# Re-ordering the w_ada sums and the output norm, and the forget gate inside the score product, in a two-block kernel on one core

## The chip, the cores and the metric

The kernel runs on one NeuronCore of one Trainium2 chip. The metric is the device time of one execution in microseconds (us). Before the change three runs gave 1096.86, 1097.15 and 1097.81 us; the median is 1097.15. About 0.2% is what a measurement can tell from no change.

## The reference

Two transformer-like layers on 256 tokens of width 1024, all in float32. What matters here:

```python
# block 1
ada = silu(c) @ w_ada + b_ada            # 6 vectors of 1024: shift, scale, gate (mixing), shift, scale, gate (FFN)
h  = rmsnorm(x) * (1 + sc1) + sh1
o  = token_mixers(h @ w_in)              # gated scan, 4 heads of 128, and a spatial gating unit (sgu)
     # o_hg = rmsnorm(o_scan) * silu(p_gate);  o_sgu = gelu(u) * (W_s LN(gelu(v)) + b)
x  = x + g1 * (o @ w_out)
h2 = rmsnorm(x) * (1 + sc2) + sh2
x  = x + g2 * conv_ffn(h2)               # w_up to 2 x 2816, 3x3 depthwise conv, gelu, w_down
x  = rmsnorm(x)
# block 2, its attention (8 heads of 64)
s  = (rms(q) . rms(k)) / 8 + cum_f[query] - cum_f[key]     # cum_f = cumsum(log_sigmoid(f))
pr = softmax(where(causal, s, -inf)) ; y = pr @ v
```

The rest of block 2 (a short convolution, a gated delta rule, three gated branches, an FFN, a last gated projection) is not touched.

## The kernel before

**GEMMs.** A weight matrix comes in blocks of 1 MB (1024 x 256), listed in `CHUNKS` in the order of use; SP loads them into a ring of three slots (`raw`). The slot of a block is free when DVE has made its low half. ACT copies a block to `whi` (`split_hi`, L575) and DVE subtracts to get `wlo` (`split_lo`, L584), both in float32r, in rings of three; activations are split in the same way (`hhi`, `hlo`). TensorE (PE) then makes three products for each 128 x 128 tile (L1067 to L1069). A block with 256 tokens is 48 such products ("rows" of the trace). A product in plain float32 shows as two rows.

**Order.** Every engine's program is written out by hand as one list, and semaphores count the steps. An engine that waits holds back all that stands behind it. PSUM banks go round in three lists: `g_units` (banks 0 and 1, GEMMs), `m_units` (banks 2 and 3, small products) and `l_units` (banks 4 to 7). A unit may start only when the unit two (or four) places ahead in its list has been emptied.

**w_ada.** The 24 blocks of w_ada give the six modulation vectors. Blocks 0 to 7 are done first. Blocks 8 to 19 are summed by DVE (`weighted_late`, L1748 to L1765: two scalings, six multiply-adds, one add, in place in the raw slot, then one add into `XC`), each at a set place of DVE's list; four of them make one of the units A2, A3, A4, where PE multiplies by ones to sum over the partitions (`ada_unit`, L1158 to L1166, eight float32 products of one column). Blocks 20 to 23 are summed by POOL (`weighted`, L539 to L547, four tensor operations) while the FFN runs, and PE makes A5 at j = 7. Each block holds a slot of the raw ring until it is summed.

**Mixing.** The scan is worked out in levels 0 to 8 between the GEMMs q, v, mv, mu. At its end come, on PE: first half of mu1, the o products (L1296 to L1301), second half of mu1, gt0, z (spatial product, L1311), the output norm's sums on0 and on1 (L1317), A3, gt1, then w_out (wo0 to wo3), A4, and the sum of squares (L1101) for the FFN's norm. DVE has the w_ada sums 15 and 16, the sgu's norm, z, the reciprocals (L1935) and products of the norm, the low halves (L1929), the splits, sums 17, 18 and 19, and after each wo unit the residual (L1950); ACT follows each residual with the squares (L777) and the next `split_hi`.

**FFN of block 1.** For j in 0 to 10: PE does fg(j), fa(j), down(j-2), 48 rows each; DVE the convolution (L1987, 16 operations) with two splits between, the product with the gelu (L2001), a third split and a low half (L2008). fa(j+1) needs the bank that L2001 empties.

**Scores of block 2.** `fox_scores` (L1427) makes, for each head and each half of the queries, two accumulating products: q with k (L1433), and a selector of 8 rows with the negative cumulated forget gates `NCF` (L1434). FQ holds the queries with the odd heads' rows zeroed, FQO those with the even heads' rows zeroed; FK holds two heads in its 128 rows. DVE takes the maxima (L2143), ACT the exponentials (L904). ACT, DVE and POOL feed this stage from head norms (`unit_norm`, L2103 to L2110).

Of the kernel before, what the change touches and what calls it, by code (L numbers as in the profile page):

```python
# [101 lines left out]
def build(nc, i, out):  # L102
# [91 lines left out]
    for j in range(FFT // 2):  # L194
        g_units += [(f"fg{j}", "act"), (f"fa{j}", "dve")] + [("A5", "dve")] * (j == 7)
# [14 lines left out]
    for lv in range(1, 7):  # L210
# [5 lines left out]
    m_units += [("oA", "act"), ("oB", "act"), ("z0", "dve"), ("z1", "dve"), ("on0", "act"), ("on1", "act"),  # L216
                ("sum1", "act"), ("sum2", "dve"), ("sum3", "dve"), ("sm", "dve"), ("colT", "dve")]
# [3 lines left out]
    with ExitStack() as ctx:  # L221
# [64 lines left out]
        acc_late = slot(12).rearrange("p (b n) -> p b n", b=4)  # L286
# [50 lines left out]
        FQO = h4(13)  # L337
# [101 lines left out]
        var_ready, rstd_ready, weigh_ready = sem("var_ready"), sem("rstd_ready"), sem("weigh_ready")  # L439
        masks_loaded, masks_ready = sem("masks_loaded"), sem("masks_ready")  # L440
        ada_late, keys_summed, vn_used = sem("ada_late"), sem("keys_summed"), sem("vn_used")
        qk_ready, d_raw, d_exp, bg_ready, coef_ready = (
# [12 lines left out]
        def _(sp):  # L455
# [24 lines left out]
            for n, (is_raw, src, (k, w)) in enumerate(CHUNKS):  # L480
# [14 lines left out]
                if is_raw:  # L495
# [7 lines left out]
                    else:  # L503
                        last.append([(ada_pool, c - 19)])
# [24 lines left out]
        def _(pool):  # L529
            pool.memset(eps, EPS).then_inc(pool_step, 1)  # L530
            pool.memset(ones_t, 1.0).then_inc(pool_step, 1)
            steps = [0]

            def link(ins):
                steps[0] += 1
                ins.then_inc(pool_link, 1)
                pool.wait_ge(pool_link, steps[0])

            def weighted(c, dst):  # L539

                n = ada_place[c]
                pool.wait_ge(raw_loaded[n % RING], 16 * (n // RING + 1))
                w = raw[:, n % RING, :].rearrange("p (k n) -> p k n", k=KT)
                link(pool.tensor_tensor(w, w, silu_c[:, :, 0:1].broadcast_to([P, KT, 256]), ALU.mult))
                link(pool.tensor_tensor(w[:, 0:4, :], w[:, 0:4, :], w[:, 4:8, :], ALU.add))
                link(pool.tensor_tensor(w[:, 0:2, :], w[:, 0:2, :], w[:, 2:4, :], ALU.add))
                pool.tensor_tensor(dst, w[:, 0, :], w[:, 1, :], ALU.add).then_inc(ada_pool, 1)  # L547

# [15 lines left out]
            for c in range(20, 24):  # L564
                weighted(c, acc_late[:, c % 4, :])
# [23 lines left out]
        def _(act):  # L589
# [168 lines left out]
            unit_act("gt0", GT[:, 0:2, :], ACT.Silu)  # L758
            split_hi(act, G["gt0"] + RING)
            for n in range(2):  # L760
# [3 lines left out]
                               scale=1.0 / P).then_inc(m_empty["act"], 1)  # L764
            for g, wait in ((2, (sgu_out, 1)), (3, (sgu_out, 2)), (0, (h_f32, 5)), (1, (h_f32, 6))):
# [68 lines left out]
            adv("fd10")  # L834
            link(act.activation(sm_coef[64:68, :], sm_log[64:68, :], ACT.Exp))
# [199 lines left out]
        def _(pe):  # L1035
# [122 lines left out]
            def ada_unit(a):  # L1158

                o = g_open(f"A{a}")  # L1160
                pe.wait_ge(*((ada_late, 4 * (a - 1)) if a < 5 else (ada_pool, 4)))
                for c in range(4 * a, 4 * a + 4):
                    for nb in range(2):
                        at = 2 * (c % 4) + nb
                        src = XC[:, c % 8, :] if a < 5 else acc_late[:, c % 4, :]
# [137 lines left out]
            gemm("mu1", 512, part=(1,))  # L1303
            gemm("gt0", 512)
# [9 lines left out]
            for n in range(2):  # L1314
                o = m_open(f"on{n}")
                pe.wait_ge(osq_ready, n + 1)
                pe.matmul(o[:, :], ones, OSQ[:, 2 * n:2 * n + 2, :].rearrange("p h t -> p (h t)"),  # L1317
                          start=True, stop=True).then_inc(m_full, 1)
# [37 lines left out]

            for j in range(FFT // 2):
# [69 lines left out]
            def fox_scores(u, a, heads):  # L1427
# [988 lines left out]
```

## Time and profile before

| what | value |
|---|---|
| median of 3 runs | 1097.15 us |
| the profiled execution | 1096.29 us, its span 1094.5 us |
| granted clock of TensorE, mean | 0.951 |
| busy: PE, PEld | 1008.1 us (92%), 952.0 us (87%) |
| busy: DVE, ACT, POOL | 783.6 us (72%), 492.5 us (45%), 48.5 us (4%) |
| chain that ended last | PE 62%, DVE 9%, ACT 3%, issue 2%, DMA 1% |
| moved by DMA | 170.56 MB, mean 156 GB/s |

The granted clock is 1 at 2.4 GHz and 0.5 at 1.2 GHz. PE busy is not PE at its peak, since matmuls are pipelined.

### The profile page before, as it was taken

How to read it: one execution, taken by the hardware profiler on the slowest of the kernel's cores; microseconds unless marked ns; L12 is line 12 of the kernel's file. 1: busy time of each engine (PE TensorE's matmuls, PEld its weight loads, DVE VectorE, ACT ScalarE, POOL GpSimd, SP SyncE). 2: the span in 40 equal slices, each digit the busy share in tenths (PEclk: the TensorE clock that was granted, in tenths of full speed). 3: DMA queues.
4: the chain of work that ended last, by engine and by line, in shares of the span. 5: the costliest groups of instructions: out<-in, count | busy, mean ns of one | idle time of the engine just before them, and what ended most of it. 6: DMA issues, size and time to landing. Idle time of an engine off the chain costs nothing.

```text
span 1094.5 us, 17756 instructions
## 1 busy us (share of the span) xinstructions
PE 1008.1 (92%) x7570; PEld 952.0 (87%) x7570; DVE 783.6 (72%) x1090; ACT 492.5 (45%) x587; POOL 48.5 (4%) x35
## 2 busy tenths in 40 slices
PE   5699999888699899969999999999999899999987
PEld 3389999787599899959888589999999799999987
DVE  5668897777989987857959376654486676666664
ACT  5545344425344444437743245232453554454452
POOL 0000000002333300000000000000000000000000
PEclk9899999798899999989998599999999899999999
DMA  9767343364366655645676364734544355555430
GB/s 340 254 222 231 106 162 119 116 205 144 128 218 197 227 179 169 170 101 113 131 167 106 63 132 115 132 95 108 124 154 154 116 186 173 184 191 193 167 104 39
DMA packets 143838, 170.56 MB, mean 156 GB/s; under 512 B 2864, under 2 KB 133184, under 8 KB 143760
## 3 DMA queue, kind: packets, MB, share of 16 engines
q1 hardware_dynamic: 142112, 165.63, 52.1%
q10 hardware_dynamic: 1200, 2.43, 0.6%
q0 software_dynamic: 448, 1.38, 0.4%
q8 instruction: 60, 0.98, 0.4%
q14 instruction: 18, 0.15, 0.0%
HBM read 168.37 MB, written 1.05 MB: 155 GB/s over the span
## 4 chain that ended last, share of the span: by engine, by line
PE 62%; DVE 9%; ACT 3%; issue 2%; DMA 1%; DVEq 0%; ACTq 0%
PE bank L1067 18%; PE bank L1069 17%; PE bank L1068 17%; PE bank L1490 4%; DVE wlo L584 2%; DVE arena L1987 2%; DMA raw<-in_w_in_dram 1%; PE bank L1434 1%; PE bank L1433 1%; ACT whi L575 1%; DVE arena L1669 1%; DVE arena L2067 1%; PE bank L1371 1%; PE bank L1101 1%; DVE arena L2106 1%
## 5 line engine op out<-in xcount | busy, mean ns | idle before, releaser
L1067 PE MATMUL bank<-hhi,whi 128*128 128x256 f32 (+1 forms) x2000 | 589.4, 295 | 54.4 <-ACT hhi L625 14.2
L1068 PE MATMUL bank<-hlo,whi 128*128 128x256 f32 (+1 forms) x2000 | 581.1, 291 | 0.0
L1069 PE MATMUL bank<-hhi,wlo 128*128 128x256 f32 (+1 forms) x2000 | 581.1, 291 | 0.0
L1067 PEld LDWEIGHTS bank<-hhi,whi 128*128 128x128 f32 x2000 | 392.6, 196 | 64.6 <-issue 59.3
L584 DVE TENSOR_TENSOR wlo<-raw,whi 128x2048 fp32r<-128x2048 f32 x131 | 304.5, 2327 | 143.2 <-ACT whi L575 118.2
L1068 PEld LDWEIGHTS bank<-hlo,whi 128*128 128x128 f32 x2000 | 392.5, 196 | 3.9 <-issue 1.2
L1069 PEld LDWEIGHTS bank<-hhi,wlo 128*128 128x128 f32 x2000 | 391.9, 196 | 2.7
L575 ACT ACTIVATE whi<-raw 128x2048 fp32r<-128x2048 f32 x131 | 250.2, 1911 | 113.9 <-PE bank L1069 97.5
L1987 DVE SCALAR_TENSOR_TENSOR arena<-arena,params 128x256 f32<-128x256 f32 x176 | 86.1, 559 | 14.0 <-ACT arena L797 14.0
L2353 DVE SCALAR_TENSOR_TENSOR arena<-bank,params,arena 128x255 f32<-128x255 f32 (+1 forms) x88 | 36.4, 476 | 33.9 <-ACT arena L1000 33.7
L897 ACT ACTIVATE arena<-bank 128x512 f32<-128x512 f32 x22 | 13.2, 598 | 96.6 <-PE bank L1069 96.6
L1000 ACT ACTIVATE arena<-bank,params 128x256 f32<-128x256 f32 x44 | 18.4, 470 | 63.1 <-PE bank L1069 63.1
L1490 PE MATMUL bank<-arena 128*128 128x128 f32 x352 | 41.8, 275 | 1.4 <-DVE arena L2230 1.4
L1490 PEld LDWEIGHTS bank<-arena 128*128 128x128 f32 x352 | 40.6, 192 | 1.6 <-DVE arena L2230 1.6
L1067 PE MATMUL bank<-whi,hhi 128*128 128x256 f32 x128 | 37.1, 290 | 0.0
L1069 PE MATMUL bank<-whi,hlo 128*128 128x256 f32 x128 | 36.2, 283 | 0.0
L1068 PE MATMUL bank<-wlo,hhi 128*128 128x256 f32 x128 | 36.2, 283 | 0.0
L777 ACT ACTIVATE arena<-XT 128x512 f32<-128x512 f32 x16 | 10.0, 631 | 47.9 <-DVE XT L1950 28.4
L1761 DVE SCALAR_TENSOR_TENSOR raw<-raw,small 128x256 f32<-128x256 f32 x72 | 29.5, 477 | 0.0
L2106 DVE RECIPROCAL arena<-arena 128x1024 f32<-128x1024 f32 x4 | 26.2, 6550 | 1.5 <-ACT arena L876 1.4
L806 ACT ACTIVATE arena<-arena 128x512 f32<-128x512 f32 x11 | 7.0, 632 | 42.2 <-DVE arena L1987 42.1
L1067 PEld LDWEIGHTS bank<-whi,hhi 128*128 128x128 f32 x128 | 24.5, 192 | 0.2 <-issue 0.2
(317 smaller groups left out, 933.9 us busy)
## 6 DMA issues: line engine op xcount, KB each, us to landing
raw<-in_w_in_dram SPq DMA_DIRECT2D x46, 1024.0 KB, 8.1
raw<-in_w_up_dram SPq DMA_DIRECT2D x44, 1024.0 KB, 5.1
raw<-in_w_down_dram SPq DMA_DIRECT2D x22, 1024.0 KB, 5.0
raw<-in_w_ada_dram SPq DMA_DIRECT2D x19, 1024.0 KB, 5.2
raw<-in_w_branch_dram SPq DMA_DIRECT2D x6, 1024.0 KB, 5.1
arena<-in_w_ada_dram SPq DMA_DIRECT2D x10, 512.0 KB, 9.0
raw<-in_w_out_dram SPq DMA_DIRECT2D x4, 1024.0 KB, 5.3
raw<-in_w_o_dram SPq DMA_DIRECT2D x4, 1024.0 KB, 5.2
```

Source lines behind the costliest of these rows:

```text
L575: act.activation(whi[:, g % RING, :], raw[:, n % RING, :], ACT.Copy).then_inc(w_hi, 1)
L584: dve.tensor_tensor(wlo[:, g % RING, :], raw[:, n % RING, :], whi[:, g % RING, :].bitcast(F32), ALU.subtract).then_inc(w_lo, 1)
L897: act.activation(dst, two(g_bank(u)), func).then_inc(g_empty["act"], 1)
L1000: ins = act.activation(acc2[:, b, n, t, :], g_bank(f"s{w}{j}")[:, T * t:T * (t + 1)], ACT.Copy, scale=col)
L1067: pe.matmul(o, wh, ah, start=start, stop=False, **kw)
L1068: pe.matmul(o, wh, al, start=False, stop=False, **kw)
L1069: return pe.matmul(o, wl, ah, start=False, stop=stop, **kw)
L1490: ins = pe.matmul(o[:, P * h:P * (h + 1)], lhsT(c, h), rhs(c, h), start=True, stop=True)
L1761: ins = dve.scalar_tensor_tensor(out=w[:, k % 2, :], in0=w[:, k, :], scalar=silu_c[:, k, 0:1], in1=w[:, k % 2, :], op0=ALU.mult, op1=ALU.add)
L1987: ins = dve.scalar_tensor_tensor(out=a, in0=pad[:, b, t, dy:dy + 4, dx:dx + 64], scalar=par("conv_w", k=FFT * tap + 2 * j + t), in1=a, op0 ...
L2106: link(dve.reciprocal(std_, std_))
L2353: ins = dve.scalar_tensor_tensor(out=acc2[:, b, n, t, d:T], in0=ps[:, T * t:T * (t + 1) - d], scalar=par("ffn_conv", k=2 * FFT * (2 - d) + ...
```

## The change

Four things. (1) The raw ring's order and DVE's list: sum 8 goes ahead of a split, sums 13 and 14 go from between the scan's levels to the gate GEMMs, 15 and 16 take their places among the levels, 17 goes ahead of a split after the sgu's norm, 18 and 19 stand each between a residual and a split. (2) on0 and on1 go ahead of gt0 in PE's list and of z in `m_units`; DVE's norm is cut into `unit_length` and `output_gate`. (3) POOL no longer sums: PE multiplies blocks 20 to 23 from the raw slot with `silu_c` itself (`ada_direct`, 16 float32 products of one column for each block), 20 and 21 ahead of fg0, 22 and 23 after fg1 and fg2; A5 becomes an `m_units` entry. (4) `NCF` goes into K: FK_EVEN and FK_ODD each hold one head's rows for k, zeros elsewhere, and in one further row the gate of the head; the queries have ones in that row. POOL clears the two, copies the eight gate rows by DMA and sets the ones; one product for each head and half is left.

```diff
-    for name in ("ff0", "ff1", "fb0", "fb1", 8, 9, "q0", 10, "q1", 11, 12, "v0", "v1", "mv0", 13, "mv1", 14, "mu0",
-                 "mu1", "gt0", "gt1", 15, "wo0", 16, "wo1", "wo2", 17, 18, "wo3", 19):
+    for name in ("ff0", "ff1", "fb0", 8, "fb1", 9, 10, "q0", 11, "q1", 12, 13, 14, "v0", "v1", "mv0", 15, "mv1", 16,
+                 "mu0", "mu1", "gt0", "gt1", 17, "wo0", "wo1", "wo2", 18, "wo3", 19):
...
+                if tag == "f" and j == 1:
+                    ada([21])
                 chunk(f"{tag}g{j}", ...)
+                if tag == "f" and j in (0, 2):
+                    ada([20 + j])
                 chunk(f"{tag}a{j}", ...)
             if j > 1:
                 chunk(f"{tag}d{j - 2}", rows(down, 2 * (j - 2)), (2, D))
-            if tag == "f" and 2 <= j < 6:
-                ada([18 + j])
+            if tag == "f" and j == 2:
+                ada([23])
...
-            for c in range(20, 24):
-                weighted(c, acc_late[:, c % 4, :])
+            pool.memset(FK_EVEN, 0.0).then_inc(fk_zero, 1)
+            pool.wait_ge(m_full, m_no("lk1") + 1)
+            pool.memset(FK_ODD, 0.0).then_inc(fk_zero, 1)
+            pool.wait_ge(rb_ready, 1)
+            pool.wait_ge(fk_zero, 2)
+            for h in range(8):
+                row = (FK_EVEN[64:65, h // 2, :], FK_ODD[0:1, h // 2, :])[h % 2]
+                pool.dma_start(row, NCF[h:h + 1, :]).then_inc(fk_rows, 16)
+            pool.wait_ge(f_ready, 1)
+            pool.memset(FQ[64:65, :, :], 1.0).then_inc(fq_rows, 1)
+            pool.memset(FQO[0:1, :, :], 1.0).then_inc(fq_rows, 1)
...
+            def ada_direct(c):
+                n = ada_place[c]
+                pe.wait_ge(raw_loaded[n % RING], 16 * (n // RING + 1))
+                w = raw[:, n % RING, :].rearrange("p (k n) -> p k n", k=KT)
+                for nb in range(2):
+                    at = 2 * (c % 4) + nb
+                    for k in range(KT):
+                        ins = pe.matmul(m_bank("A5")[:, at:at + 1], w[:, k, P * nb:P * (nb + 1)], silu_c[:, k, 0:1],
+                                        start=k == 0, stop=k == KT - 1)
+                ins.then_inc(m_full if c == 23 else ada_read, 1)
+            ada_direct(20)
+            ada_direct(21)
             for j in range(FFT // 2):
                 gemm(f"fg{j}", T, 8 if j == 0 else None)
+                if j in (1, 2):
+                    ada_direct(21 + j)
                 gemm(f"fa{j}", T)
-                if j == 7:
-                    ada_unit(5)
...
-                    q, k = (FQ, FQO)[h % 2][:, h // 2, P * a:P * (a + 1)], FK[:, h // 2, 0:n]
-                    pe.matmul(o[:, n * m:n * (m + 1)], q, k, start=True, stop=False)
-                    ins = pe.matmul(o[:, n * m:n * (m + 1)], sel(0, h), NCF[0:8, 0:n], start=False, stop=True)
+                    q, k = (FQ, FQO)[h % 2][:, h // 2, P * a:P * (a + 1)], (FK_EVEN, FK_ODD)[h % 2][:, h // 2, 0:n]
+                    ins = pe.matmul(o[:, n * m:n * (m + 1)], q, k, start=True, stop=True)
                 ins.then_inc(l_full, 1)
             pe.wait_ge(f_ready, 2)
+            pe.wait_ge(fk_rows, 128)
+            pe.wait_ge(fq_rows, 2)
```

DVE's list at the end of mixing, after the sgu's norm (the names are those of the code; "sum" is `weighted_late`, "split" is `split_lo`):

```text
before: split(wo0) sum16 split(wo1) z0 z1 modulation3 [norm0 low2 gate0] [norm1 low3 gate1] split(wo2) low0 low1
        sum17 sum18  res0 split(wo3) sum19  res1 split(fg0)  res2 split(fa0)  res3
after:  sum17 split(wo0) norm0 z0 z1 split(wo1) low2 low3 norm1 modulation3 gate0 gate1 low0 low1 split(wo2)
        res0 sum18 split(wo3)  res1 sum19 split(fg0)  res2 split(fa0)  res3
```

DVE's list under the gate GEMMs: before `split sum8 sum9 split decay sum10 split sum11 sum12 split(v0)`, after `sum8 split sum9 sum10 split decay sum11 split sum12 sum13 sum14 split(v0)`. DVE writes K as two operations on 64 partitions each, in place of one on 128. ACT waits for `wsm_zero` before a small exponential, and takes the norm's roots ahead of gt0.

## Rows read from the trace of the kernel before

**Rows 1.** The page, part 2: TensorE's granted clock in 40 slices of 27.4 us, tenths.

```profile
PEclk9899999798899999989998599999999899999999
```

**Rows 2.** Busy time by stretch: start:end, length, then PE, PEld, DVE, ACT, POOL busy (instructions), granted clock, DMA share, GB/s.

```profile
195.00:257.00 62.00, 47.90 (x310) 43.97 (x308) 46.38 (x75) 22.25 (x25) 4.88 (x11) 0.84 0.53 175
257.00:300.00 43.00, 32.02 (x243) 31.11 (x244) 38.12 (x55) 18.15 (x25) 11.29 (x6) 0.90 0.38 118
300.00:400.00 100.00, 96.15 (x766) 95.63 (x765) 92.55 (x115) 45.00 (x50) 31.06 (x12) 0.96 0.63 211
430.00:470.00 40.00, 40.00 (x336) 40.00 (x335) 31.21 (x44) 18.64 (x19) 0.00 (x0) 1.00 0.65 179
...
199.40:213.00 13.60, 12.27 (x45) 10.16 (x46) 8.50 (x13) 3.69 (x5) 0.00 (x0) 0.50 0.45 147
...
602.20:629.40 27.20, 27.20 (x67) 15.66 (x68) 8.69 (x32) 7.06 (x25) 0.00 (x0) 0.50 0.31 62
```

**Rows 3.** Timeline of PE, matmuls: start, time, line, instructions [idle before and its releaser].

```profile
200.73 3.78 PE L1317 MATMUL bank<-arena,cf 128*128 128x512 f32 x4 [3.75 <-DVE arena L1918]
204.30 3.41 PE L1166 MATMUL bank<-cf,XT 128*128 128x1 f32 x16
...
246.29 1.84 PE L1166 MATMUL bank<-cf,XT 128*128 128x1 f32 x16
...
257.33 0.55 PE L1067 MATMUL bank<-hhi,whi 128*128 128x256 f32 x1 [5.38 <-DVE hlo L1684]
...
299.30 0.55 PE L1067 MATMUL bank<-hhi,whi 128*128 128x256 f32 x1 [8.88 <-DVE arena L2001]
```

**Rows 4.** Timeline of DVE, one w_ada sum: its first and its last instruction.

```profile
92.38 0.61 DVE L1758 TENSOR_SCALAR raw<-raw,small 128x256 f32<-128x256 f32 x2
...
95.39 0.43 DVE L1765 TENSOR_TENSOR XT<-raw 128x256 f32<-128x256 f32 x1
```

**Rows 5.** Timeline of DVE at the end of mixing: a split, a reciprocal, a split, the last residual.

```profile
191.96 2.29 DVE L584 TENSOR_TENSOR wlo<-raw,whi 128x2048 fp32r<-128x2048 f32 x1 [4.58 <-ACT whi L575]
...
207.84 3.34 DVE L1935 RECIPROCAL arena<-arena 128x512 f32<-128x512 f32 x1
...
241.39 2.29 DVE L584 TENSOR_TENSOR wlo<-raw,whi 128x2048 fp32r<-128x2048 f32 x1 [2.56 <-issue]
...
249.23 0.87 DVE L1950 SCALAR_TENSOR_TENSOR XT<-bank,mod,XT 128x256 f32<-128x256 f32 x2
```

**Rows 6.** Timeline of ACT: the high half of block v0.

```profile
99.04 1.91 ACT L575 ACTIVATE whi<-raw 128x2048 fp32r<-128x2048 f32 x1
```

**Rows 7.** The page, part 6: loads of w_in, KB each, median us to landing.

```profile
raw<-in_w_in_dram SPq DMA_DIRECT2D x46, 1024.0 KB, 8.1
```

**Rows 8.** Timeline at the FFN's start: POOL's multiplication, and DVE's split beside it.

```profile
283.09 3.93 POOL L544 TENSOR_TENSOR raw<-raw,small 128x2048 f32<-128x2048 f32 x1 [25.17 <-DMA raw<-in_w_ada_dram]
...
287.22 4.48 DVE L584 TENSOR_TENSOR wlo<-raw,whi 128x2048 fp32r<-128x2048 f32 x1
```

**Rows 9.** The chain that ended last, in order of time: start, us, engine, line.

```profile
471.46 0.89 DVE XT L1950 x2
...
623.02 1.15 PE bank L1434 x2
...
685.46 1.78 PE bank L1490 x16
...
848.57 3.47 PE bank L1101 x16
```

**Rows 10.** Timeline of the scores: the first product, then the weight loads of two later ones.

```profile
597.63 0.38 PE L1433 MATMUL bank<-arena 128*128 128x128 f32 x2
...
614.89 0.50 PEld L1433 LDWEIGHTS bank<-arena 128*128 128x128 f32 x2 [0.65 <-issue]
...
616.05 0.50 PEld L1434 LDWEIGHTS bank<-arena,XT 8*128 8x128 f32 x2 [0.65 <-issue]
```

**Rows 11.** Waits of the whole span: total us, times, longest us.

```profile
DVE arena L2143 <- PE bank L1434: 19.3, 6, 3.8
```

More of the change, by code:

```diff
@@ L503, in _ @@
                     else:
-                        last.append([(ada_pool, c - 19)])
+                        last.append([(ada_read, c - 19) if c < 23 else (m_full, m_no("A5") + 1)])
                     n_ada = max(n_ada + 1, 8) if n_ada >= 5 else n_ada + 1
@@ L764, in _ @@
                                scale=1.0 / P).then_inc(m_empty["act"], 1)
+            unit_act("gt0", GT[:, 0:2, :], ACT.Silu)
+            split_hi(act, G["gt0"] + RING)
             for g, wait in ((2, (sgu_out, 1)), (3, (sgu_out, 2)), (0, (h_f32, 5)), (1, (h_f32, 6))):
@@ L834, in _ @@
             adv("fd10")
+            act.wait_ge(wsm_zero, 3)
             link(act.activation(sm_coef[64:68, :], sm_log[64:68, :], ACT.Exp))
@@ L1303, in _ @@
             gemm("mu1", 512, part=(1,))
+            for n in range(2):
+                o = m_open(f"on{n}")
+                pe.wait_ge(osq_ready, n + 1)
+                pe.matmul(o[:, :], ones, OSQ[:, 2 * n:2 * n + 2, :].rearrange("p h t -> p (h t)"),
+                          start=True, stop=True).then_inc(m_full, 1)
             gemm("gt0", 512)
@@ L1313, in _ @@
                 ins.then_inc(m_full, 1)
[L1314 to L1318, printed above, removed]
             ada_unit(3)
@@ L1868, in _ @@
             level(2)
-            weighted_late(13)
+            weighted_late(15)
             values(0, 1)
@@ L1908, in _, with mixed_low, unit_length, output_gate @@
             dve.tensor_tensor(MV, MV, sgu_b.unsqueeze(1).broadcast_to([P, 2, 512]), ALU.add).then_inc(vn_ready, 1)
+            weighted_late(17)
             split_lo(dve, G["mu1"] + RING)
-            weighted_late(16)
-            split_lo(dve, G["gt0"] + RING)
+            def mixed_low(g):
+                dve.wait_ge(h_hi, 4 + (3, 4, 1, 2)[g])
+                s = slice(2 * g, 2 * g + 2)
+                dve.tensor_tensor(mix_lo[:, s, :], OM[:, s, :], mix_hi[:, s, :].bitcast(F32), ALU.subtract
+                                  ).then_inc(h_lo, 1)
+            def unit_length(n):
+                s = slice(2 * n, 2 * n + 2)
+                dve.wait_ge(*m_done(f"on{n}"))
+                link(dve.reciprocal(hrstd[:, s, :], hstd[:, s, :]))
+                link(dve.tensor_tensor(OM[:, s, :], OM[:, s, :], hrstd[:, s, :], ALU.mult))
+            def output_gate(n):
+                dve.wait_ge(*g_done(f"gt{n}"))
+                for h in (2 * n, 2 * n + 1):
+                    ins = dve.scalar_tensor_tensor(out=OM[:, h, :], in0=OM[:, h, :], scalar=par("hg_norm", k=h),
+                                                   in1=GT[:, h, :], op0=ALU.mult, op1=ALU.mult)
+                ins.then_inc(h_f32, 1)
+            unit_length(0)
             for n in range(2):
@@ L1923, in _ @@
                 dve.tensor_tensor(o, o, U[:, 2 * n:2 * n + 2, :], ALU.mult).then_inc(sgu_out, 1)
+            split_lo(dve, G["gt0"] + RING)
+            mixed_low(2)
+            mixed_low(3)
+            unit_length(1)
             modulation(3, g_wait("A3"), g_empty["dve"])
-            def mixed_low(g):
-                dve.wait_ge(h_hi, 4 + (3, 4, 1, 2)[g])
-                s = slice(2 * g, 2 * g + 2)
-                dve.tensor_tensor(mix_lo[:, s, :], OM[:, s, :], mix_hi[:, s, :].bitcast(F32), ALU.subtract
-                                  ).then_inc(h_lo, 1)
-            for n in range(2):
-                s = slice(2 * n, 2 * n + 2)
-                dve.wait_ge(*m_done(f"on{n}"))
-                link(dve.reciprocal(hrstd[:, s, :], hstd[:, s, :]))
-                link(dve.tensor_tensor(OM[:, s, :], OM[:, s, :], hrstd[:, s, :], ALU.mult))
-                mixed_low(2 + n)
-                if n == 1:
-                    dve.wait_ge(*g_done("gt1"))
-                for h in (2 * n, 2 * n + 1):
-                    ins = dve.scalar_tensor_tensor(out=OM[:, h, :], in0=OM[:, h, :], scalar=par("hg_norm", k=h),
-                                                   in1=GT[:, h, :], op0=ALU.mult, op1=ALU.mult)
-                ins.then_inc(h_f32, 1)
-            split_lo(dve, G["gt1"] + RING)
+            output_gate(0)
+            output_gate(1)
             mixed_low(0)
             mixed_low(1)
+            split_lo(dve, G["gt1"] + RING)
             def residual(nb, ps, gate):
@@ L2009, in _ @@
                                   ).then_inc(u_lo, 1)
-                if j == 7:
-                    modulation(5, g_wait("A5"), g_empty["dve"])
+                if j == 3:
+                    dve.wait_ge(m_full, m_no("A5") + 1)
+                    modulation(5, m_bank("A5"), m_empty["dve"])
             split_lo(dve, G["fd9"] + RING)
             dve.wait_ge(down_used, FFT // 2)
+            dve.wait_ge(*m_done("A5"))
             for c in range(4):
@@ L2133, in _ @@
             dve.wait_ge(*g_done("fk1"))
-            unit_norm(FK, fk_std, "sfk1", par("fox_gain", k=1), f_ready)
+            dve.wait_ge(*m_done("sfk1"))
+            dve.wait_ge(fk_zero, 2)
+            link(dve.reciprocal(fk_std, fk_std))
+            for dst, r in ((FK_EVEN, slice(0, 64)), (FK_ODD, slice(64, 128))):
+                ins = dve.scalar_tensor_tensor(out=dst[r, :, :], in0=FK[r, :, :], scalar=par("fox_gain", k=1)[r, :],
+                                               in1=fk_std[r, :, :], op0=ALU.mult, op1=ALU.mult)
+            ins.then_inc(f_ready, 1)
             adv("scc0")
```

48 lines of the change are left out of this document (17 added, 31 removed).

## Prediction

> **What bounds the kernel now.** I read the page first, where the clock slices are lowest at about 600 us [rows 1], then the busy time by stretch, then the gaps of TensorE in the timeline. TensorE is the bound: in the middle of the first block's FFN it is busy without a break, 336 rows in 40.00 us, so 0.119 us for one row of a GEMM [rows 2]. The time that can be won is therefore what TensorE loses elsewhere: in waits, and in stretches where the granted clock is at 1.2 instead of 2.4 GHz. By stretch: the end of mixing (195 to 257 us) has 14.1 us without a matmul and clock 0.84; the FFN's start (257 to 300) 11.0 us without one; 300 to 400 us another 3.9; and 602 to 629 us runs wholly at the half clock though PE never stops [rows 2].
>
> **End of mixing.** PE waits 3.75 us for DVE before the output norm's sums (L1317), because they follow z in the bank order and DVE is in a w_ada sum; the clock then is at half for 13.6 us, so the norm sums and A3 run slowly [rows 2, 3]. Then VectorE sets the end: it carries sums of 3.44 us (first to last instruction [rows 4]), splits of 2.29, reciprocals of 3.34, and waits 2.56 us for ScalarE before a split that follows a residual; its last residual begins at 249.23 [rows 5].
>
> The new order, from the split at 191.96 on (durations as in rows 5, small steps 0.7 to 0.9 each): split, wait for the norm's root, first unit length (4.0) to 198.0; z twice 3.2 to 201.2; split 203.5; two low parts 204.9; second unit length 208.9; modulation and two output gates 210.9; two low parts 212.3; split 214.6. TensorE, without gaps at 0.119 a row, has wo0 ready at 215.6. Residual 216.5; sum and split 222.2; residual and sum 226.6; split (its block asked for only when sum 18 frees its slot) 229.3; residual 230.1; ScalarE and split 235.0; last residual from 235.8. That is 13.4 us earlier than 249.23. Here sums 18 and 19 cover two of the 2.56 us waits, sum 17 lies where DVE waited for ScalarE, and 15 and 16 are in places that 13 and 14 held.
>
> **Earlier sums.** Those two, 13 and 14, now stand ahead of the split of V's first block. Their DVE work (6.9) was free under the gate GEMMs only up to ScalarE's split of v0 at 99.04 [rows 6]. The queue asks for v0 one sum (3.4) later and a w_in load takes 8.1 us by the median [rows 7]; ScalarE waits in order, with the masks and q0 behind it; DVE's decayed queries come about 3.5 us later, and the first V GEMM 2.7 later. Between 0 and 6.9, I take 2.7: nothing after it on TensorE has a gap to absorb it before 178 us. So mixing gives -10.7. The norm's sums ahead of gt0 cost PE nothing new: their squares are made right after the o products, and mu1's second half lies between. ScalarE's new wait (wsm_zero) and DVE's last one (A5) are for things done long before.
>
> **w_ada 20 to 23.** POOL's four blocks go. While POOL multiplies (3.93 us), a split on DVE takes 4.48 instead of 2.29 [rows 5, 8]; that made fa2 wait 8.88 us at 299.30 [rows 3]. From the end of the sum of squares (251.95, which is 257.33 less its wait of 5.38 [rows 3]) to the end of the down products at 471.46 [rows 9] are 219.5 us; 11 x 144 rows at 0.119 are 188.5, so 31.0 us are lost there. In their place come 64 full-height fp32 products of one column. The nearest row is ada_unit: 8 such products (16 rows) took 1.84 us at full clock and 3.41 at half, so 0.23 or 0.43 each [rows 3]. All at full clock: 14.7; all at half: 27.3. Blocks 20 and 21 stand in the 5.38 us wait for normalise. What one-column products do to the clock no row shows for long: A3's were at half, and the clock stayed at half in the stretch that they shared with GEMM rows [rows 2, 3]. I take the half clock for most of them, as for A3: 11.1 us for 20 and 21 (13 products at 0.23, 19 at 0.43), 4.5 each for 22 and 23, three stretches at half clock afterwards (5.1), 1.6 of small waits: 26.8, so -4.2. Bounds: +1 (all at half, longer stretches) and -14.3 (all at full: 14.8 and 1.9). DVE is no longer the bound of fa1 and fa2: a split loses 2.2 us to POOL, the conv groups beside it as much again or more, and without that the bank is free before PE, now later itself, wants it. The loads of fg1 and fg2 now wait for PE to free slots 20 and 21; in the order of the list they land about as they are needed, which I put at under 1 us and rival five at more.
>
> **Scores.** 16 of 32 products go, those with 8 rows. Now two products alternate at 1.15 us for 256 columns at the half clock, 597.6 to 624.2 us in all [rows 9, 10]. Products of full height cost 0.22 (128 columns: 8 in 1.78) and 0.43 (256: 8 in 3.47) at full clock [rows 9]. I take these for the new ones, which all have one shape: 8 x 0.22 + 8 x 0.43 = 5.2 us. DVE waited 19.3 us for the scores [rows 11], and ScalarE's exponentials wait for DVE. With 5.2 us on TensorE the maxima follow each other; of the 19.3 about 19 go, and scv1, whose first 5.2 us ran at half clock (624.2 to 629.4 [rows 2, 9]), gains 2.6: -22 with rounding, as the exponentials and two splits still set the second p_ready. Bounds: -14 (each left-over product as dear as now) and -24.
> DVE writes K in two halves of 64 partitions instead of one op: 1.3 us later, but PE is at scv0 until then. The eight row copies on POOL's queue start after lk1; nine GEMM blocks of 5.7 us lie between that and the scores, some 50 us, for eight copies of 1 KB rows. The memsets on POOL have the same cover; if either came late, PE would stand still before the first score (rival four).
>
> The Trainium skill ("TensorE: Matmul & The Clock Gate", section on LDWEIGHTS) says that a load takes its time from the columns of the weights and not from the rows of contraction. On the load the trace agrees: 0.50 us for 8 rows and for 128 [rows 10]. Read as a rule for the whole product it makes the 8-row product no dearer or cheaper than its neighbour; dropping it would then halve the stretch and no more, 13 us instead of 5.2.
>
> **Sum.** -10.7 - 4.2 - 22.0 = -36.9 against the profiled execution's 1096.29 (span 1094.5 and 1.8 around it): 1059.4. The median of the runs is 0.86 above it: 1060.3, so 1060.
>
> **Rivals.**
> One: one-column products leave the clock at 2.4 GHz. For: A4's ran at full clock behind GEMM rows [rows 3]. Against: A3's. FFN -14.3 instead of -4.2: 1050. Chance 0.22.
> Two: the 16 score products keep 0.42 and 1.15 us, since the alternation is not what makes them dear. For: both kinds of product show the same spacing now. Against: full-height ones elsewhere [rows 9]. Half of 26.5 is 13 us for the scores, DVE and ScalarE hide little: -14 instead of -22: 1068. Chance 0.13. (The page named above leads to the same.)
> Three: the end of mixing gives half, because blocks 19, fg0 and fa0 land later than 5 us among the residuals and each residual waits for its split: +6, 1066. Chance 0.12.
> Four, the other side: POOL's row copies. They stand in order behind lk1, PE waits for all eight before the first score. They decide from the moment at which they land more than 37 us after PE is ready for them, about 100 us after they are issued; at 120 us the time is 1117 with 20 us lost net. Against: w_in's loads of 1 MB, the slow ones of the page, land in 8.1 us [rows 7]. Chance 0.02.
> Five: it does not do what it says: the gaps at the FFN's start only change their name, from DVE to the raw slots, as fg1 and fg2 are asked for only behind PE's products: a gap of one load, 5 to 8 us, before each: 1070. Chance 0.06.
>
> **Chances.** Forecast 0.45, the five rivals 0.55. 1046 to 1074 holds one, two, three and five with their bounds; left out are four and sums of several misses, near 0.2 together. A measurement of this kernel tells about 0.2% from no change, 2.2 us. All cases but four lie far below; with what I may have missed: faster 0.95, same 0.02, slower 0.03.
>
> **What would show it.** L1433 x32 alone in the scores, under 7 us from first to last, no clock 0.5 at 602 to 629; the wait at L1317 gone; last residual of mixing near 239; the four direct sums 4 to 7 us each, at clock 0.5 for the first two; no 8.88 us wait; the down products end near 457. I am wrong if v0's split pushes the levels by over 5 us, if the direct sums stand at 0.23 each, or if PE waits for fk_rows.

## The result, and the profile after

The new kernel takes 1058.87 us (median of 4 runs, 1054.66 to 1061.12), the kernel before in the same rounds 1097.01: a ratio of 0.9667, 95% interval 0.9638 to 0.9696. The forecast was 1060. With the same code the four runs lie 0.6% apart, so a single run is less sharp than the 0.2% given at the top. The profiled execution took 1058.56 us, its span 1056.8, with a mean granted clock of 0.971 (0.951 before). PE is busy for 991.1 us (1008.1 before), DVE 760.7, POOL 14.8 (48.5 before). The chain that ended last is now 76% PE.

Five points in both traces show where the 37.7 us of span went:

| point | before | after | shift | forecast |
|---|---|---|---|---|
| first o product | 179.27 | 181.22 | +1.95 | +2.7 |
| end of the sum of squares, mixing's end | 251.95 | 242.59 | -9.36 | -10.7 |
| end of the down products | 471.43 | 457.88 | -13.55 | -14.9 |
| PE goes on after scb1 (yf) | 649.38 | 613.75 | -35.63 | -36.9 |
| end of the span | 1094.5 | 1056.8 | -37.7 | -36.9 |

The last 2.07 us come behind the scores: a stretch of 3.41 us at half clock at 649.94 is gone (1.7 us), and one wait of PE is 4.82 us instead of 5.19.

The page's clock slices of the new kernel, in tenths, as in [rows 1]:

```profile
PEclk9999999996899999989999999999999999999999
```

The dip at 600 us is gone; one at the FFN's start has come, deeper than before. The busy time by stretch of the new kernel, in the columns of [rows 2]:

```profile
195.00:246.00 51.00, 47.31 (x360) 45.67 (x358) 40.13 (x57) 19.91 (x22) 3.35 (x5) 0.94 0.45 146
246.00:293.00 47.00, 47.00 (x317) 47.00 (x318) 32.48 (x58) 19.59 (x26) 3.38 (x9) 0.77 0.63 202
302.00:400.00 98.00, 98.00 (x819) 98.00 (x818) 78.86 (x114) 46.67 (x49) 0.00 (x0) 1.00 0.56 182
242.40:254.90 12.50, 12.50 (x65) 12.48 (x64) 8.35 (x17) 4.30 (x10) 6.73 (x13) 0.55 0.63 193
260.60:277.60 17.00, 17.00 (x146) 17.00 (x145) 12.30 (x21) 8.25 (x11) 0.00 (x0) 1.00 0.44 130
583.00:592.00 9.00, 7.71 (x53) 6.88 (x52) 8.90 (x32) 1.71 (x9) 0.00 (x0) 1.00 0.53 129
602.00:629.00 27.00, 24.40 (x208) 23.43 (x208) 18.32 (x23) 12.16 (x14) 0.76 (x1) 1.00 0.67 153
```

From 246 to 400 us PE has no break; what is lost at the FFN's start is clock, 0.77. From 302 to 400 VectorE is busy for 78.86 us of 98, where it was busy for 92.55 of 100. The timeline of PE in the new kernel, at mixing's end and in the FFN:

```profile
191.22 1.88 PE L1305 MATMUL bank<-arena,cf 128*128 128x512 f32 x4
...
200.47 1.84 PE L1164 MATMUL bank<-cf,XT 128*128 128x1 f32 x16
...
210.90 0.35 PE L1065 MATMUL bank<-hhi,whi 128*128 128x256 f32 x1 [2.72 <-ACT whi L572]
...
242.42 12.63 PE L1365 MATMUL bank<-small,raw 128*128 128x1 f32 x64
254.92 0.56 PE L1065 MATMUL bank<-hhi,whi 128*128 128x256 f32 x1
...
274.75 4.17 PE L1365 MATMUL bank<-small,raw 128*128 128x1 f32 x32
...
292.88 3.63 PE L1365 MATMUL bank<-small,raw 128*128 128x1 f32 x32
```

The norm sums (L1305) start without a wait and take 1.88 us at full clock where they took 3.78 [rows 3]; A3's sums take 1.84 where they took 3.41. New is a wait of 2.72 us before wo0, and blocks 20 and 21 (L1365, 64 records for 32 products) hold PE for 12.5 us at clock 0.55, while 23 takes 3.63 at full clock and 22 4.17, of which the last 1.3 us are at half clock. The scores in the same view:

```profile
584.10 3.67 PE L1446 MATMUL bank<-arena 128*128 128x128 f32 x24
589.07 1.99 PE L1446 MATMUL bank<-arena 128*128 128x256 f32 x8 [1.29 <-DVE small L2170]
590.71 0.47 PE L1065 MATMUL bank<-hhi,whi 128*128 128x256 f32 x1
```

16 products, 6.96 us from first to last, 1.29 of them a wait for the maxima (a group's name takes the form of its first: it holds eight products of 128 columns and four of 256). VectorE's 19.3 us of waits for the scores [rows 11] are gone. In the waits of the whole span, ScalarE's for the maxima, before and then (second fence) now:

```profile
ACT arena L904 <- DVE small L2152: 24.7, 2, 13.3
```

```profile
ACT arena L902 <- DVE small L2179: 8.1, 1, 8.1
```

VectorE at mixing's end in the new kernel, its timeline:

```profile
206.42 3.34 DVE L1936 RECIPROCAL arena<-arena 128x512 f32<-128x512 f32 x1
...
210.52 0.17 DVE L1667 TENSOR_TENSOR mod<-bank,params 128x8 f32<-128x8 f32 x1
...
219.80 0.88 DVE L1971 SCALAR_TENSOR_TENSOR XT<-bank,mod,XT 128x256 f32<-128x256 f32 x2 [3.94 <-PE bank L1067]
...
239.87 0.87 DVE L1971 SCALAR_TENSOR_TENSOR XT<-bank,mod,XT 128x256 f32<-128x256 f32 x2
```

The first residual is at 219.80, the last at 239.87 (249.23 before [rows 5]).

### The profile page after: what moved, and what is told of

It reads as the page before. It is cut to its first block, busy times and chain, and to the rows that moved or that the text cites. A ratio compares the mean times of both kernels' runs of the same rounds, so it can differ in the third digit from the quotient of the medians.

```text
span 1056.8 us, 17913 instructions
## 1 busy us (share of the span) xinstructions
PE 991.1 (94%) x7650; PEld 951.4 (90%) x7650; DVE 760.7 (72%) x1091; ACT 491.6 (47%) x586; POOL 14.8 (1%) x31
## 4 chain that ended last, share of the span: by engine, by line
PE 76%; DVE 12%; ACT 4%; DMA 3%; issue 2%; SPq 1%; DVEq 0%
PE bank L1065 21%; PE bank L1066 21%; PE bank L1067 21%; PE bank L1504 4%; DVE wlo L581 3%; ACT whi L572 2%; DMA raw<-in_w_in_dram 2%; PE bank L1365 2%; PE bank L1117 2%; PE bank L1260 1%; DVE arena L2127 1%; DMA raw<-in_w_ada_dram 1%; DVE arena L2088 1%; SPq L478 1%; DVE arena L1683 1%
## 5 line engine op out<-in xcount | busy, mean ns | idle before, releaser
L1065 PEld LDWEIGHTS bank<-hhi,whi 128*128 128x128 f32 x2000 | 388.5, 194 | 41.7 <-issue 31.3
L581 DVE TENSOR_TENSOR wlo<-raw,whi 128x2048 fp32r<-128x2048 f32 x131 | 299.5, 2289 | 140.6 <-ACT whi L572 111.5
L1066 PEld LDWEIGHTS bank<-hlo,whi 128*128 128x128 f32 x2000 | 388.6, 194 | 3.8 <-issue 1.2
L572 ACT ACTIVATE whi<-raw 128x2048 fp32r<-128x2048 f32 x131 | 250.3, 1912 | 122.1 <-PE bank L1067 104.6
L2006 DVE SCALAR_TENSOR_TENSOR arena<-arena,params 128x256 f32<-128x256 f32 x176 | 71.5, 477 | 25.7 <-ACT arena L794 25.7
L1065 PE MATMUL bank<-whi,hhi 128*128 128x256 f32 x128 | 37.7, 294 | 0.0
L1066 PEld LDWEIGHTS bank<-wlo,hhi 128*128 128x128 f32 x128 | 25.1, 196 | 0.2 <-issue 0.2
L1067 PEld LDWEIGHTS bank<-whi,hlo 128*128 128x128 f32 x128 | 25.0, 195 | 0.0
```

The costliest lines, as they stand in the source:

```text
L572: act.activation(whi[:, g % RING, :], raw[:, n % RING, :], ACT.Copy).then_inc(w_hi, 1)
L581: dve.tensor_tensor(wlo[:, g % RING, :], raw[:, n % RING, :], whi[:, g % RING, :].bitcast(F32), ALU.subtract).then_inc(w_lo, 1)
L1065: pe.matmul(o, wh, ah, start=start, stop=False, **kw)
L1066: pe.matmul(o, wh, al, start=False, stop=False, **kw)
L1067: return pe.matmul(o, wl, ah, start=False, stop=stop, **kw)
L2006: ins = dve.scalar_tensor_tensor(out=a, in0=pad[:, b, t, dy:dy + 4, dx:dx + 64], scalar=par("conv_w", k=FFT * tap + 2 * j + t), in1=a, op0 ...
```

## The experiments

Each run was made beside the kernel before on the same chip, and not all on the same chip; so times are compared by their ratios to it, and stretches within the traces.

**1. The scores alone.**

```diff
-                    pe.matmul(o[:, n * m:n * (m + 1)], q, k, start=True, stop=False)
-                    ins = pe.matmul(o[:, n * m:n * (m + 1)], sel(0, h), NCF[0:8, 0:n], start=False, stop=True)
+                    ins = pe.matmul(o[:, n * m:n * (m + 1)], q, k, start=True, stop=True)
```

> The kernel before with one part of the change alone: the forget gate as a row of K, one score product for each head instead of two. Theory (the 8-row products and their neighbours are what is dear, and the exponentials wait for them): the stretch of the scores falls from 26.5 us to under 7 us, no half clock in it, 22 us faster than before, about 1075. Rival (the left-over products stay at 0.42 and 1.15 us): stretch of 13 us, 14 us faster, about 1083. Rival (part of the gain in the new kernel came from the other parts, through the clock): 18 us or less.

Measured: 1071.76 us against 1094.86, ratio 0.9786 (0.9770 to 0.9802), so 23.1 us of the 37.7. The scores go from 595.64 to 602.60, all at clock 1.00. Theory held; both rivals fall.

**2 and 3. Why the old products were dear.** Run 2 leaves their number and sorts them within a bank; run 3 takes the new kernel and issues each product twice.

```diff
-                    pe.matmul(o[:, n * m:n * (m + 1)], q, k, start=True, stop=False)
+                    pe.matmul(o[:, n * m:n * (m + 1)], q, k, start=m == 0, stop=False, skip_group_check=True)
+                for m, h in enumerate(heads):
...
```

```diff
+                    pe.matmul(o[:, n * m:n * (m + 1)], q, k, start=True, stop=True)
                     ins = pe.matmul(o[:, n * m:n * (m + 1)], q, k, start=True, stop=True)
```

> The kernel before, with all its 32 score products, but in each bank the full-height products first and then the 8-row ones, instead of one of each in turn. Theory (it is the change from one height to the other, product by product, that makes both dear): some 10 to 13 us for the stretch instead of 26.5, 12 us faster than before, about 1085. Rival (an 8-row product is dear by itself, wherever it stands): full-height ones at 0.22 and 0.43, 8-row ones still 0.42 and more; stretch about 16 us at full clock. Rival (neither order nor height matters, it is the number of products): no change, 1097.

> The new kernel with each score product issued twice, both of full height, the second over the first: 32 products again, of one shape. Theory (shape, not number): 16 x 0.22 + 16 x 0.43 = 10.4 us for the stretch instead of 5.2, about 5 us slower than the new kernel, 1064. Rival (number): 0.42 and over for each product, stretch 20 us or more, with the half clock back: 15 to 22 us slower, 1074 to 1081.

Measured: sorted, 1085.04 us, ratio 0.9907 (0.9875 to 0.9938), and the stretch of the scores falls from 26.5 us to 20.1 only, where 10 to 13 were expected; doubled, 1061.01 us, ratio 0.9696 (0.9676 to 0.9717), some 3 us over the new kernel (5 expected; the wait of 1.29 us for the maxima is gone in it). Timeline of PE, sorted:

```profile
597.47 1.05 PE L1433 MATMUL bank<-arena 128*128 128x128 f32 x8
598.45 1.15 PE L1435 MATMUL bank<-arena,XT 8*128 8x128 f32 x8
599.54 1.16 PE L1433 MATMUL bank<-arena 128*128 128x128 f32 x8
600.62 1.15 PE L1435 MATMUL bank<-arena,XT 8*128 8x128 f32 x8
601.71 1.84 PE L1433 MATMUL bank<-arena 128*128 128x256 f32 x4
603.48 2.07 PE L1435 MATMUL bank<-arena,XT 8*128 8x256 f32 x4
605.48 2.08 PE L1433 MATMUL bank<-arena 128*128 128x256 f32 x4
```

and the busy time by stretch, first sorted, then (second fence) doubled:

```profile
602.20:622.00 19.80, 19.80 (x53) 13.21 (x52) 7.50 (x30) 7.06 (x25) 0.00 (x0) 0.50 0.42 81
```

```profile
581.00:592.00 11.00, 11.00 (x71) 10.17 (x70) 8.65 (x32) 4.49 (x17) 0.00 (x0) 1.00 0.62 161
```

One group of four products of 128 columns follows the other after 1.09 us, whichever height it has: 4 x 0.22 and 0.2 for the change. In turns each product paid that change: 0.22 + 0.2 = 0.42, the old spacing. At half clock a group of two of 256 columns takes 2.00: 2 x 0.86 and 0.29; in turns 0.86 + 0.29 = 1.15, again the old one. So an 8-row product costs what a full one does, and the change of height costs 0.2 us at full clock and 0.29 at half. (With the height the operands change too; but the new kernel alternates between two tiles of queries and two of K, and its products follow each other at 0.22.) 32 products of one height take 10.6 us at full clock (expected 10.4). With the same number and columns the clock stays at 1.00 with full heights only, but with 8-row products in half of them it is at 0.50 for 20.48 us sorted and for 27.31 in turns. All four traces with 8-row score products (before, and runs 2, 9 and 10) fall to half clock within the scores, and none of the ten others does. So the order explains the changes of height and not the clock, which is why sorting won less than expected. By an estimate from these rows, the old 26.5 us are 5.2 for the products that remain, 5.2 for those that go, some 6 for 31 changes of height (31 x 0.2), and the rest, some 10, clock. The Trainium skill ("TensorE: Matmul & The Clock Gate", section on LDWEIGHTS) says a load's time follows its columns and not its rows. This case agrees for the load, 0.50 us at both heights [rows 10], and run 2 shows 0.22 us at both heights for the product too.

**4. Modulation ahead of the second unit length.**

```diff
+            modulation(3, g_wait("A3"), g_empty["dve"])
             unit_length(1)
-            modulation(3, g_wait("A3"), g_empty["dve"])
```

> The new kernel with VectorE's modulation(3) ahead of the second unit length instead of behind it. Theory: wo0 takes the bank that A3's sums held, VectorE gives it back only at 210.69 because a reciprocal of 3.34 us stands ahead of the modulation, and this is PE's new wait of 2.72 us at 208.18: without it all of mixing's end comes 2.5 us earlier, about 1056.4. Rival: the residuals are bound by the loads of 18, 19 and the first FFN blocks, so the 2.7 us come back as a wait for raw blocks: 1058.9, no change.

Measured: 1057.09 us, ratio 0.9658 (0.9643 to 0.9672): not to be told from the new kernel's. The trace shows more. DVE and PE there:

```profile
204.19 0.16 DVE L1667 TENSOR_TENSOR mod<-bank,params 128x8 f32<-128x8 f32 x1
204.26 3.34 DVE L1936 RECIPROCAL arena<-arena 128x512 f32<-128x512 f32 x1
```

```profile
200.00:229.00 29.00, 28.99 (x241) 28.79 (x241) 26.77 (x41) 9.42 (x10) 0.00 (x0) 1.00 0.54 173
```

The bank comes free at 204.35 and PE works without a break to 229, so the 2.72 us are gone. The profile had put that wait down to ScalarE's split (L572), which wo0 does not need: that is the event that came last. From the first o product to the end of the sum of squares six traces with the order of the change take 61.4, 63.0, 61.2, 62.7, 61.4 and 61.7 us, three with the modulation first 59.6, 59.3 and 58.3: 2.8 us less on the mean. In this run's profile most of it is lost again: its FFN ran 28.3 us at half clock, more than any other, and took 217.4 us (table below). The medians of runs 5 and 8, which differ in this order alone and were made in the same rounds, tell it better: 1048.81 and 1044.73 us, 4.1 us. So the rival (the residuals are bound by loads) falls.

**5 and 6. The direct sums.** Run 5 gives 21 to 23 back to VectorE; run 6 leaves out 14 of the 16 products of each of 20 and 21.

```diff
-            ada_direct(21)
...
-                if j in (1, 2):
-                    ada_direct(21 + j)
...
+                if j == 6:
+                    pe.wait_ge(ada_late, 15)
+                    for c in range(21, 24):
...
+                if 2 <= j < 5:
+                    weighted_late(19 + j)
```

```diff
-            ada_direct(20)
-            ada_direct(21)
+            for c in (20, 21):
...
+                    ins = pe.matmul(m_bank("A5")[:, at:at + 1], w[:, 0, P * nb:P * (nb + 1)], silu_c[:, 0, 0:1],
+                                    start=True, stop=True)
```

> The new kernel with blocks 21, 22 and 23 summed by VectorE at the end of the FFN's turns 2, 3 and 4 (their eight steps as for blocks 8 to 19, 6 one-column products on PE behind fa6), and only block 20 as direct products in the wait for normalise. Theory: VectorE is busy only some 31 us of 40 there, so its 3 x 3.44 us are covered, and PE gets back what 21 (6.3 us at half clock), 22 and 23 (3.63 each), and the half clock behind them cost: 10 to 14 us faster than the new kernel, 1045 to 1049. Rival (VectorE becomes the bound of those turns, as it was before the change): 3 to 10 us come back as PE's waits for splits, 1052 to 1056. Rival (the half clock comes anyway, when PE waits for normalise): 8 us.

> The new kernel with 14 of the 16 direct products of each of the blocks 20 and 21 left out (two of one column stay, so that the slots come free in the same way; the second FFN gate of those columns is then wrong). It prices what these products cost beside the wait that covers them. Theory: they end at 255.06, and PE could go on at about 248 to 250, so 5 to 7 us, and the half clock behind them is due to them, 2.8 more: 8 to 9 us faster, about 1050. Rival (the clock drops anyway, since PE then waits 5 to 8 us for normalise): 5 us, 1054.

Measured: 1048.81 us, ratio 0.9582 (0.9556 to 0.9608), and 1054.34 us, ratio 0.9630 (0.9603 to 0.9657). Run 5, busy time by stretch, then PE's timeline:

```profile
300.00:400.00 100.00, 100.00 (x836) 100.00 (x835) 90.91 (x149) 48.48 (x53) 0.00 (x0) 1.00 0.63 210
```

```profile
240.78 3.63 PE L1364 MATMUL bank<-small,raw 128*128 128x1 f32 x32
246.32 0.55 PE L1064 MATMUL bank<-hhi,whi 128*128 128x256 f32 x1 [1.91 <-DVE hlo L1702]
```

VectorE is busy for 91% and PE never waits for it from 300 to 400: no bound. (Between 268 and 283 us PE does wait for it, 2.1 us in all.) Block 20 is free: the FFN's first row comes 5.38 us after the sum of squares, as in run 6 and before, against 12.33 in the new kernel. Block 21 and the slow clock thus cost 7 us there, 22 and 23 another 7.8. These sizes scatter with the clock: in the five traces with both blocks the first row comes 9.2 to 13.3 us after the sum of squares, and in run 8, where block 20 alone ran at half clock, 6.5. The FFN, sum of squares to down products, takes 204.0 us in run 5 and 208.9 in run 6.

Against the new kernel's ratio, run 5 wins 9 us, just under the 10 to 14 expected, and run 6 wins 4, which is its rival's 5 and not the theory's 8 to 9. The trace says why: without 28 of the 32 products of blocks 20 and 21 the half clock comes all the same, at 242.60, 1.2 us after the sum of squares, for 10.24 us (17.07 at 243.53 in the new kernel). It comes in run 5 too, at 245.38 for 6.83 us.

The same stretch in five traces whose FFN has the same code shows what scatters: it is the time at half clock.

| run | half clock in the FFN | FFN |
|---|---|---|
| doubled scores | 17.1 | 212.2 |
| early sums cut | 17.1 | 212.1 |
| new kernel | 23.9 | 215.3 |
| new kernel again | 27.3 | 216.9 |
| modulation first | 28.3 | 217.4 |

11.2 us more at half clock, 5.3 more in time. The mean is 214.8; run 5 is 10.8 below it and run 6 5.9.

**7. The early sums.**

```diff
-                for k in range(KT):
+                for k in range(2 if c in (13, 14) else KT):
```

> The new kernel with VectorE's sums of blocks 13 and 14 cut to two of their eight steps (loads, slots and order unchanged; those columns of the mixing gate are wrong), so 4.9 us less work on VectorE ahead of the split of v0. Theory: it is this work that pushes the levels by 1.95 us: level 8 ends near 179.3 again and the time is 1057, 1.9 us less. Rival: the shift comes from the loads, which stand in the new order, or from the half clock at 117 us: no change, 1058.9.

Measured: 1059.11 us, ratio 0.9669 (0.9646 to 0.9692); first o product at 179.82. The theory falls: less work in these sums brings nothing that can be told from the scatter. Over the other traces the first o product is at 179.27, 179.09, 179.19, 178.60 and 178.71 with the old order in front (mean 179.0), and at 181.22, 179.46, 179.00, 179.72, 178.70, 180.20, 181.26 and 179.48 with the new one (mean 179.9). The earlier sums cost about 0.9 us. ScalarE and then PE in the new kernel, and (third line) ScalarE in run 7, in their timelines:

```profile
100.72 1.91 ACT L572 ACTIVATE whi<-raw 128x2048 fp32r<-128x2048 f32 x1 [1.68 <-DMA raw<-in_w_in_dram]
...
115.46 3.20 PE L1260 MATMUL bank<-arena 128*128 128x128 f32 x16 [0.69 <-DVE arena L1817]
...
99.30 1.91 ACT L572 ACTIVATE whi<-raw 128x2048 fp32r<-128x2048 f32 x1 [1.78 <-DMA raw<-in_w_in_dram]
```

Block v0 is now asked for at 95.73 us instead of 92.49 and lands at 100.70; ScalarE waits for it, and waits as long in run 7, where VectorE has less to do (that trace runs 1.4 us earlier as a whole). VectorE's decayed queries (L1817) end 1.7 us later than before, and PE waits for them for 0.69 to 0.81 us in all nine new traces, in none of the old. So it is the load, as the rival of this run had it. In six of the nine a stretch of 3.41 us at half clock follows near 116 us; their o products start at 180.3 on the mean, those of the three without it at 179.1. That stretch was not tried by itself.

**8. Both together**, and the same beside the new kernel in five rounds:

> The new kernel with the modulation ahead of the second unit length and with blocks 21 to 23 on VectorE. If the two gains are independent they add up: theory 1042 to 1047, 12.5 to 16.5 us faster than the new kernel. If the residuals are bound by loads, the first adds nothing: as the version with the sums on VectorE alone.

> The new kernel unchanged, on the same chip and in the same rounds as the next one, for a direct comparison; it also shows how far the FFN's time, the half clock in it and the start of the o products scatter with the same code. Theory: o products start at 179 to 181, so that the earlier sums cost 0.5 us rather than 2; the FFN takes 212 to 217 us. Time 1057 to 1060.

> The version with the modulation ahead of the second unit length and blocks 21 to 23 on VectorE, beside the new kernel. Expected: 12 to 14 us faster than the new kernel beside it, about 1045; mixing's end (o products to sum of squares) 59.5 us instead of 61.9, FFN 204 instead of 214.

Measured: 1044.73 us, ratio 0.9543 (0.9520 to 0.9566), by the ratios 13.6 us faster than the new kernel, as the sum of the two gains would have it; then the new kernel 1060.59 us, ratio 0.9694 (0.9661 to 0.9727), and the version beside it 1045.67 us, ratio 0.9557 (0.9528 to 0.9586): 15 us, 1.4%, faster than the new kernel (12 to 14 expected) and 49 faster than the one before. Its mixing's end takes 59.3 and 58.3 us, its FFN 204.4 and 203.8.

**9 and 10. What POOL's sums cost before.** On the kernel before: three of POOL's four steps cut; then the same three done on a scratch buffer, behind the addition that gives the slot back.

```diff
-                link(pool.tensor_tensor(w, w, silu_c[:, :, 0:1].broadcast_to([P, KT, 256]), ALU.mult))
-                link(pool.tensor_tensor(w[:, 0:4, :], w[:, 0:4, :], w[:, 4:8, :], ALU.add))
-                link(pool.tensor_tensor(w[:, 0:2, :], w[:, 0:2, :], w[:, 2:4, :], ALU.add))
                 pool.tensor_tensor(dst, w[:, 0, :], w[:, 1, :], ALU.add).then_inc(ada_pool, 1)
```

```diff
                 pool.tensor_tensor(dst, w[:, 0, :], w[:, 1, :], ALU.add).then_inc(ada_pool, 1)
+                w = slot(8, 2).rearrange("p (k n) -> p k n", k=KT)
+                link(pool.tensor_tensor(w, w, silu_c[:, :, 0:1].broadcast_to([P, KT, 256]), ALU.mult))
...
```

> The kernel before with POOL's four w_ada sums in the FFN cut to the last of their four steps (blocks 20 to 23 are still loaded and their slots given back, by one addition of 256 columns; the second FFN gate is wrong). Theory: VectorE's splits fall back from 4.5 to 2.3 us in that stretch, the waits of 8.88 and 3.41 us are gone, and the FFN takes about 204 us instead of 219.5 from the sum of squares to the down products: 15 us faster than before, about 1081. Rival: the waits there are of another cause, no change.

> As the run with POOL's sums cut, but POOL does the three steps that were cut on a scratch buffer behind the addition, four times, so it works as much as before while the raw slots come free at once. Theory A (POOL's work slows VectorE's splits beside it): splits of 4.5 us come back and with them most of the loss, about 1090 or more. Rival B (what cost was that POOL held raw slots for some 10 us each, so that the next blocks landed late): no slower than with the sums cut, about 1081.

Measured: cut, 1078.72 us, ratio 0.9858 (0.9825 to 0.9891), 15.5 us faster; on scratch, 1095.67 us, ratio 1.0011 (0.9992 to 1.0030): all of it back. Groups of VectorE from 280 to 400 us (count, then busy us and mean ns), cut and then on scratch:

```profile
L1984 DVE SCALAR_TENSOR_TENSOR arena<-arena,params 128x256 f32<-128x256 f32 x114 | 46.9, 482 | 15.8 <-ACT arena L794 15.8
L581 DVE TENSOR_TENSOR wlo<-raw,whi 128x2048 fp32r<-128x2048 f32 x20 | 45.7, 2286 | 4.6 <-issue 2.3 <-ACT whi L572 2.2
L2005 DVE TENSOR_TENSOR hlo<-arena,hhi 128x512 fp32r<-128x512 f32 x7 | 4.8, 685 | 0.7 <-ACT hhi L809 0.7
L1998 DVE TENSOR_TENSOR arena<-bank,arena 128x512 f32<-128x512 f32 x7 | 4.8, 681 | 0.0
```

```profile
L1991 DVE SCALAR_TENSOR_TENSOR arena<-arena,params 128x256 f32<-128x256 f32 x104 | 60.5, 651 | 5.5 <-ACT arena L800 5.5
L587 DVE TENSOR_TENSOR wlo<-raw,whi 128x2048 fp32r<-128x2048 f32 x18 | 42.3, 2350 | 2.8 <-ACT whi L578 2.3 <-issue 0.5
L2012 DVE TENSOR_TENSOR hlo<-arena,hhi 128x512 fp32r<-128x512 f32 x6 | 9.7, 1621 | 0.7 <-ACT hhi L815 0.7
L2005 DVE TENSOR_TENSOR arena<-bank,arena 128x512 f32<-128x512 f32 x6 | 4.1, 680 | 0.0
```

The 104 conv steps grow from 0.482 to 0.651 us, 17.6 us in all, the low parts from 0.685 to 1.621. The means hide how it is spread: the 12 conv steps that ran beside POOL took 2.0 us each, up to 3.8, and all others 0.48. PE's wait before fa2 is 7.3 us on scratch, 0.8 cut, 8.9 before. So it was the work of POOL beside VectorE, not the slots that it held. The last group stays at 0.68 us, also in the two of its instructions that ran beside POOL: it reads PSUM and one buffer of SBUF, while the others read two of SBUF. This is what the Trainium skill says ("SBUF — State Buffer", Who interferes with whom): a VectorE instruction with two SBUF inputs contends with a GpSimd one that reads SBUF, one with at most one SBUF input, outside the modes that use both ports, does not. The trace agrees: 1.621 against 0.685 us for the low parts, 0.68 in both for the group with PSUM.

## Why the prediction was right, point by point

**Scores** (-22.0): right in size and mechanism. -22.1 from the down products to yf, 23.1 alone. The stretch is 6.96 us instead of 5.2, since the maxima of the first banks now hold up the second half by 1.29 (in runs 5 to 7 they do not, and it is 5.4 to 5.5); the half clock is gone. Rival two (the products keep their dear price, 1068) fell with runs 1 and 3: what was dear was the change of height (run 2) and the half clock that stood in every trace with 8-row score products. In front of scc1 PE now waits 2.87 us for VectorE's copy of fv1 (L2143); the old trace has no wait there but 6.83 us at half clock from 574.85 on, so little is won by that clock.

**FFN** (-4.2): the stretch took 215.3 us, the 26.8 of loss that I had put down exactly, but the terms are off and cancel. Blocks 20 and 21: 12.33 us to the first row, forecast 11.1, nearly all at half clock. 22 and 23: 3.63 each at full clock, forecast 4.5 (the half clock that 22 ran into is in the next term). At 0.23 us a product they show what I had named as a sign of being wrong; it holds for these two and not for 20 and 21. Half clock afterwards: 5.68 us at 254.92 and 6.83 at 277.66, 6.3 us lost, forecast 5.1. That sums to 12.3 + 7.3 + 6.3 = 25.9, and 0.9 of the rest. The table under runs 5 and 6 says that the hit is partly luck: the same code gives 212 to 217. That the direct products bring the half clock, as I had it, is not shown (run 6). Rival one (full clock, 1050) fell, rival five (gaps at the raw slots) too: PE has no break. What I had under "a split loses 2.2 us to POOL, the conv groups as much again or more" is borne out by runs 9 and 10, and is bigger: 15.5 us of time. One reading was off: POOL's multiplication ended at 287.02, so the split of 4.48 at 287.22 stood beside POOL's additions, and beside the multiplication stood a conv step of 3.84. With POOL's sums cut the FFN takes 205.4 us, 14.1 less than before; the direct products gave 9.9 of that back.

**Mixing's end** (-13.4 net of the shift): -11.3 (9.36 and 1.95). The step that failed is "TensorE, without gaps at 0.119 a row, has wo0 ready at 215.6". With the shift of 1.95 it would be 217.6; it came at 219.8, as wo0 takes the bank of A3, and the new order puts A3's modulation behind a reciprocal. I counted the modulation's 0.2 us on VectorE and not who waits for it. Run 4 shows 2.8 us for it. From the start of the first residual to that of the last 20.1 us passed, forecast 20.2 (215.6 to 235.8). The wait at L1317 is gone as forecast. Rival three (half of the gain, loads late) is not what happened: ScalarE's waits for blocks there are 1.44 and 0.80 us. No run has the new order of this stretch alone, so its gain is read from the traces: 58.3 to 63.0 us in nine with the new order, 70.9 to 72.7 in five with the old.

**Early sums** (+2.7, of 0 to 6.9): +1.95 in the profiled execution, 0.9 over all traces, and not by VectorE's work (run 7). The mechanism, the queue asking for v0 one sum later and ScalarE behind it, is borne out: it is asked for 3.24 us later. The sizes are not: the block landed in 4.97 us and not in 8.1, so ScalarE was 1.7 us late and the decayed queries 1.7, forecast 3.5; the first V GEMM does not wait, PE waits 0.69 us before the scan's products at 115.46.

**Rival four**, slower: POOL issued its eight row copies from 521.95 on, and the first score came at 584.10 without a wait; it was never near. The cover was 62 us, where I had some 50.

## What to carry to other kernels

Price a helper engine by what it does to its neighbour: POOL's sums, 41 us of an engine without a share of its own in the page's chain, cost 15.5 us through VectorE. When an operation moves within an engine's order, ask which bank or slot it gives back and who opens that next; the profile may name another event. A wait can be filled with work exactly as long as it lasts: one block in 5.4 us of wait was free at full clock, the second cost 7 us in the new kernel.

## What was not expected of the hardware

A change between 8-row and 128-row products costs 0.2 us each time at full clock, on top of either (run 2). One-column fp32 products take 0.23 us each at full clock. In the new kernel the half clock came at 243.53, 1.1 us after the start of blocks 20 and 21, and left at 260.60, 5.68 us of GEMM rows after their end. That they bring it is not shown: in run 5 block 20 ran at full clock and the half clock came behind it, in runs 4 and 8 it came over 1.9 us before the first of them, and in run 6 it came without 28 of the 32. What grows with them is its length, 10.24 us in run 6 and 17.07 in the new kernel. With the same code the time at half clock in the FFN ranged from 17.1 to 28.3 us from run to run, which is why single profiles differ there by 5 us. Behind the FFN it is as much: two profiles of the new kernel have 21.3 and 43.1 us at half clock there, and take 598.9 and 605.0 us.
